# Eight chunk sums of a conditioning matrix moved from TensorE to VectorE, other quarters of the PE array for odd 64x64 matrices, and new woven orders, in a two-block fp32 trunk

## The reference, cut to what matters

```python
shift, scale, gate = jnp.split(jax.nn.silu(c) @ p['w_ada'] + p['b_ada'], 3, axis=-1)
shift_c, scale_c, gate_c = jnp.split(jax.nn.silu(c_ctx) @ p['w_ada'] + p['b_ada'], 3, axis=-1)
h = x * (1.0 + scale[:, None, :]) + shift[:, None, :]
...
sol = lax.linalg.triangular_solve(eye + lmat, rhs, left_side=True, lower=True, unit_diagonal=True)
```

## Time and profile before

| | |
|---|---|
| median of 3 runs | 1589.13 us (1587.75 to 1591.42) |
| profiled execution, its own time | 1589.21 us |
| its span in the profile | 1587.4 us |
| granted TensorE clock over the span | 0.997 |
| TensorE busy | 1547.7 us, 97% |
| VectorE / ScalarE / GpSimd busy | 612.0 / 390.3 / 198.6 us |

### The profile page before, as it was taken

How to read it: one execution, slowest core, us unless ns; L and a number is a source line. 1 busy time by engine, 2 the same in 40 slices (tenths; PEclk the granted TensorE clock), 3 DMA queues, 4 the chain that set the end, 5 groups by cost and what they waited for, 6 DMA issues and landing times.

```text
span 1587.4 us, 18219 instructions
## 1 busy us (share of the span) xinstructions
PE 1547.7 (97%) x7512; PEld 1017.6 (64%) x7512; DVE 612.0 (39%) x1394; ACT 390.3 (25%) x750; POOL 198.6 (13%) x274
## 2 busy tenths in 40 slices
PE   6999999999999999999999999999999999999997
PEld 2544544455444444464876888588888858889873
DVE  1332433464100001423344412265678216567721
ACT  1122325323100000031226320144223213422320
POOL 0321200221010011113011202110100011010000
PEclk9999999999999999999999999999999999999999
DMA  8732222302022222241331243424221434232231
GB/s 356 271 158 106 107 106 106 133 27 79 1 80 79 80 106 92 80 178 53 129 134 63 102 183 134 153 107 155 107 108 55 161 121 154 107 130 85 88 125 40
DMA packets 17366, 184.16 MB, mean 116 GB/s; under 512 B 2306, under 2 KB 2818, under 8 KB 4740
## 3 DMA queue, kind: packets, MB, share of 16 engines
q1 hardware_dynamic: 17284, 183.01, 30.3%
HBM read 181.95 MB, written 1.05 MB: 115 GB/s over the span
## 4 chain that ended last, share of the span: by engine, by line
PE 95%; ACT 3%; DVE 1%; DMA 1%; issue 1%; SPq 0%; POOLq 0%; POOL 0%; ACTq 0%
PE ps L688 91%; PE ps L743 3%; DMA arena<-in_wf 1%; DVE arena L1613 0%; ACT arena L1227 0%; ACT L1567 0%; ACT L1565 0%; DVE arena L1610 0%; DVE arena L1607 0%; ACT arena L1440 0%; ACT arena L1565 0%; ACT arena L1456 0%; ACT L1458 0%; ACT L1456 0%; ACT arena L1567 0%
## 5 line engine op out<-in xcount | busy, mean ns | idle before, releaser
L688 PE MATMUL ps<-arena 128*128 128x256 f32 (+9 forms) x7020 | 1498.9, 398 | 27.6 <-DMA arena<-in_wf 11.2
L688 PEld LDWEIGHTS ps<-arena 128*128 128x128 f32 (+6 forms) x7020 | 963.8, 177 | 529.3 <-issue 422.6
L2161 POOL TENSOR_TENSOR arena<-arena 128x256 f32<-128x256 f32 (+5 forms) x214 | 164.0, 786 | 936.0 <-DVE arena L1613 575.9
L1613 DVE SCALAR_TENSOR_TENSOR arena<-arena 128x256 f32<-128x256 f32 (+4 forms) x455 | 212.9, 524 | 139.5 <-ACT arena L1369 38.8
L1613 DVE SCALAR_TENSOR_TENSOR arena<-arena,ps 128x256 f32<-128x256 f32 (+2 forms) x136 | 64.6, 482 | 397.7 <-PE ps L688 292.7
L1227 ACT ACTIVATE arena<-ps 128x512 f32<-128x512 f32 (+2 forms) x216 | 110.0, 523 | 354.3 <-PE ps L688 315.4
L1607 DVE TENSOR_TENSOR arena<-arena 128x512 f32<-128x512 f32 (+14 forms) x156 | 92.1, 612 | 115.2 <-ACT arena L1227 39.9
L743 PEld LDWEIGHTS ps<-arena 128*128 128x128 f32 x488 | 55.8, 141 | 30.4 <-issue 20.5
L1395 ACT ACTIVATE arena<-ps 128x512 f32<-128x512 f32 (+1 forms) x24 | 13.5, 562 | 248.5 <-PE ps L688 248.5
L743 PE MATMUL ps<-arena 128*128 128x128 f32 x488 | 71.3, 277 | 3.2 <-ACT arena L1474 1.5
L1610 DVE TENSOR_SCALAR arena<-arena 128x256 f32<-128x256 f32 (+9 forms) x181 | 62.9, 383 | 15.7 <-POOL arena L2161 10.8
(11 more groups left out here) (92 smaller groups left out, 289.5 us busy)
## 6 DMA issues: line engine op xcount, KB each, us to landing
arena<-in_wf SPq DMA_DIRECT2D x69, 2048.0 KB, 8.1
arena<-in_wf SPq DMA_DIRECT2D x22, 1024.0 KB, 6.9
arena<-in_wf SPq DMA_DIRECT2D x2, 1152.0 KB, 7.8
arena<-in_xinT SPq DMA_DIRECT2D x2, 1024.0 KB, 16.1
arena<-in_xin SPq DMA_DIRECT2D x4, 512.0 KB, 3.9
arena<-in_rp SPq DMA_DIRECT2D x2, 1024.0 KB, 8.5
arena<-in_consts SPq DMA_DIRECT2D x1, 1410.0 KB, 19.1
arena<-in_pa SPq DMA_DIRECT2D x2, 532.0 KB, 10.0
```

Source lines behind the costliest of these rows:

```text
L688: return e.matmul(o, l, r, start=start, stop=stop, skip_group_check=True)
L1613: return e.scalar_tensor_tensor(out=o, in0=x, scalar=s, in1=y, op0=op0, op1=op1)
L2161: return e.tensor_tensor(o, x, y, op)
```

## The change

1. The products of the later eight ada pieces leave TensorE. VectorE multiplies each of the 8 chunks of a piece (128x512) by a per-partition scalar and adds it up, for each of the two rows: 16 instructions for a piece, 2 `tensor_scalar` and 14 `scalar_tensor_tensor`, into `ACC`, four tiles of 128x512 in `X`. They are cut into four parts of four instructions (`ep`), put into the four steps after the place where `ef` stood. TensorE turns the four blocks of both sums (`es`, `et`: 8 transposes for a piece where there were 4), two pieces later; VectorE reduces and adds the bias once for each row. ScalarE's copy goes. The weights of the piece are done with only when VectorE's last part is.
2. In the inverse, odd matrices use the other two quarters of the array (upper rows to lower outputs and the reverse) and a second PSUM bank, so four matmuls on four quarters follow each other. Fourteen of the sixteen groups of a layer are so changed (t0 to t5, y0 to y3, x0 to x3). Each copy and each predicated copy becomes two of 128x256 (or four of 64x256). Four matmuls of 128 columns with 64 stationary columns are added for the swapped halves of `wt`.
3. `ORDER_A[0]` and `ORDER_A[1]` are new strings with the same counts of letters. `ORDER_B` is unchanged.

```diff
 ORDER_A = [
-    "daadddddaaddaddddadadgaaadgadgaadgdgaagdagadagadgadagadgagadgaadgadaaggadaaaggadggaadggagadgagdgaaddgaggadgggaa"
-    "dgagdagdagdggadgdgaadgaagadagaagdadgaadgadagddaadaaaddaaadaagagadgaaaggagadgagagagadgadaggdaggggg",
+    "dddddddddaaddadadadadaagdggdagdddadgaadadgadaadaggaagaagdaagagdagadaggddgaaaaaggaadggadgadagaaggagdadgadaagag"
+    "adgagggdaaagggdgdaaaadgaagdaaagdgdadagdaadagddaadaddggagdgagagagadggaagagaadgaaggaadggaagggaggggd",
...
 def dense_a(l):
-        return ([("es", k - 1, "V")] if k else []) + ([("ef", k, "A")] if k < len(ADA_LATER) else [])
+        turn = [k - 2] if 2 <= k < 8 else [6, 7] if k == 8 else []
+        return [(n, i, "V") for i in turn for n in ("es", "et")] + ([("ef", k, "-")] if k < len(ADA_LATER) else [])
...
+    for i, step in enumerate(list(steps)):
+        for n, k, _ in step:
+            if n == "ef":
+                for q in range(4):
+                    steps[i + 1 + q] = steps[i + 1 + q] + [("ep", 4 * k + q, "-")]
+    steps = [[g for g in step if g[0] != "ef"] for step in steps]
...
             for n, (l, j) in enumerate(ADA_LATER):
-                out[f"a{l}ada{j}"] = dense_done(0, "ef", n)
+                out[f"a{l}ada{j}"] = ada_acc.at(0, n)
...
                 b = bank("wt", l)
                 for d in range(2):
                     p.wait_ge(de_iv.at(l, IV_W + d))
+                    for j in range(2):
+                        mm(b[HALVES[j], 256 + 128 * d:384 + 128 * d], W16[:, d, 4 - 4 * j:8 - 4 * j, :], ident, d == 0, True)
...
+                def quarters(o):
+                    return [(o + n, HALVES[j], HALVES[1 - j if n else j]) for n in range(2) for j in range(2)]
...
-                        b = bank("y", l, k)
-                        for i in range(8):
-                            for x in HALVES:
-                                ins = mm(b[x, 64 * i:64 * i + 64], NL[x, 8 * d + i, x], XM64[x, 8 * d + i, :], i == 0, True)
+                        b = [bank("y", l, k, n) for n in range(2)]
+                        for i in range(4):
+                            for o, x, z in quarters(8 * d + 2 * i):
+                                ins = mm(b[o % 2][z, 64 * i:64 * i + 64], NL[x, o, x], XM64[x, o, :], i == 0, True)
...
+            def ada_parts(k, q):
+                l, j = ADA_LATER[k]
+                w = weights(f"a{l}ada{j}", 8)
+                v.wait_ge(pieces[f"a{l}ada{j}"][2], dense_dve(0, "ps", 3))
+                if k > 1 and q == 0:
+                    v.wait_ge(dense_done(0, "et", k - 2))
+                for kk in (2 * q, 2 * q + 1):
+                    for r in range(2):
+                        acc = ACC[k % 2][r]
+                        if kk == 0:
+                            ins = ts(acc, w[:, kk, :], cs3[:, kk, r:r + 1], None, ALU.mult)
+                        else:
+                            v.wait_ge(acc_made[r])
+                            ins = stt(acc, w[:, kk, :], cs3[:, kk, r:r + 1], acc, ALU.mult, ALU.add)
...
-                        copy(Y64[:, 8 * d:8 * d + 8, :], r3(psum("y", l, k), 8)).then_inc(de_yc.hit(l, k), 1)
+                        for n in range(2):
+                            ins = copy(Y64[:, 8 * d + n:8 * d + 8:2, :], r3(psum("y", l, k, n)[:, 0:256], 4))
+                        ins.then_inc(de_yc.hit(l, k), 1)
...
```

More of the change, by code:

```diff
@@ L209, in build_program @@
         PT4 = [X[:, 0:512], X[:, 512:1024]]
+        ACC = [[X[:, 1024 * i + 512 * r:1024 * i + 512 * r + 512] for r in range(2)] for i in range(2)]
         cs3 = r3(cs, 8)
@@ L341, in after @@
         def after(e, *per):
-            return Ev(e.sem, *per, start=sum(e.per))
+            return Ev(e.sem, *per, start=e.base[0] + sum(e.per))
         def landed(e, l=0):
@@ L349, in build_program @@
         pt_zero = after(cs_ready, 2)
+        ada_acc = ev("ada_acc", 8)
         DENSE = [dense_a(l) for l in range(2)]
-        FLAT = [[g for step in s for g in step if g[0] != "hx"] for s in DENSE]
+        FLAT = [[g for step in s for g in step if g[0] not in ("hx", "ep")] for s in DENSE]
         FIRST = [("pf", 0, "A"), ("pf", 1, "A"), ("ps", 0, "V"), ("ps", 1, "V"), ("pf", 2, "A"), ("pf", 3, "A"),
@@ L1104, in delta @@
                         p.wait_ge(de_yc.at(l, k), de_tc.at(l, k))
-                        b = bank("x", l, k)
-                        for i in range(8):
-                            for x in HALVES:
-                                ins = mm(b[x, 64 * i:64 * i + 64], XT64[x, 8 * d + i, :], Y64[x, 8 * d + i, :], i == 0, True)
+                        b = [bank("x", l, k, n) for n in range(2)]
+                        for i in range(4):
+                            for o, x, z in quarters(8 * d + 2 * i):
+                                ins = mm(b[o % 2][x, 64 * i:64 * i + 64], XT64[z, o, :], Y64[z, o, :], i == 0, True)
                         ins.then_inc(de_x.hit(l, k), 1)
@@ L1115, in delta @@
                 yield
-                b = bank("y", l, 4)
+                b = bank("y", l, 4, 0)
                 for i in range(8):
@@ L1123, in delta @@
                 p.wait_ge(de_yc.at(l, 4), de_tc.at(l, 5))
-                b = bank("x", l, 4)
+                b = bank("x", l, 4, 0)
                 for i in range(8):
@@ L1547, in delta @@
                 a.wait_ge(de_y.at(l, 4))
[L1548 removed]
+                copy(Y64[:, 0:8, :], r3(psum("y", l, 4, 0), 8)).then_inc(de_yc.hit(l, 4), 1)
                 yield
@@ L1624, in ada_sum, with ada_turned @@
                     ).then_inc(dn_dve.hit(0, BY_DVE[0][(g, n)]), 1)
+            acc_made = [None, None]
+            def ada_parts(k, q):
[12 more added lines that the diff above has]
+                            ins = stt(acc, w[:, kk, :], cs3[:, kk, r:r + 1], acc, ALU.mult, ALU.add)
+                        if (kk, r) != (7, 1):
+                            ins.then_inc(v.own(), 1)
+                            acc_made[r] = v.now()
+                        else:
+                            ins.then_inc(ada_acc.hit(0, k), 1)
+            def ada_turned(k, r):
+                l, j = ADA_LATER[k]
+                g = ("es", "et")[r]
+                v.wait_ge(dense_done(0, g, k), landed(d_bada, l))
+                a4 = AS[:, 4 * r:4 * r + 4]
+                e.tensor_reduce(a4, r3(psum("dense", 0, g, k), 4), AX, ALU.add).then_inc(v.own(), 1)
+                v.wait_ge(v.now())
+                stt(r3(SCOL[l], 24)[:, 4 * j:4 * j + 4, r], a4, 1.0 if j in (2, 3) else 0.0,
+                    BADA[:, 24 * l + 4 * j:24 * l + 4 * j + 4], ALU.add, ALU.add
+                    ).then_inc(dn_dve.hit(0, BY_DVE[0][(g, k)]), 1)
+                v.wait_ge(dense_dve(0, g, k))
             def dense(l):
```

102 lines of the change are left out of this document (53 added, 49 removed).

## The result

The changed kernel takes **1592.97 us** (median, 1590.57 to 1595.44) beside 1588.85 of the kernel before on the same chip: ratio 1.0026, interval 1.0018 to 1.0035. It is slower by 4.1 us, just over what such a measurement tells from no change. The prediction said 1584, faster by some 5 us. Its range holds the result; its likeliest case and its direction do not.

The account below looks back on a forecast made before the run. It took TensorE's work, busy 1547.7 of 1587.4 us, plus few idle stretches as the bound. Terms -10 + 10 - 0.5 - 5.4 = -5.9 us gave 1583.3, rounded to 1584; 8-in-10 range 1574 to 1597 us.

Parts of the forecast that it names:

- likeliest case: Whole kernel: all terms as forecast, 1584 us, faster than before; chance 0.48.
- 3. Orders: Layer A0's new strings: some idle may go, the new tail waits some 1.5 us; -0.5 us for both.
- The bound of +2: Upper bound in us for `ORDER_A[1]`, said only to permute work in which TensorE hardly idles; lower bound -1, taken as 0.
- The ada products, -10 us: TensorE in A0: eight pieces' products go, 14.6 us, and 32 transposes are added, 4.7 us; work falls by 10 us.
- VectorE's sums, +10 us: A0: later ring loads make TensorE wait before gg, su and sv; at least 7.0 us, at most 20, taken as +10.
- The chain there is load, TensorE, load: Why A0's added load waits would hide against nothing else; used for the +10 us of VectorE's sums.
- forecast 12.0: A0: next piece's load lands 12.0 us behind the TensorE group, after VectorE's part (2.5 us) and the load (8.1 us).
- forecast 9.8: A0, ag to gg: TensorE's letters between the last ag group and the gg piece take 9.8 us.
- The quarters, -5.4 us: Inverses of two layers: four quarters at work shorten the groups, net of wt's added matmuls; -2.7 us a layer.
- The first rival: Inverse: two quarters still set the pace, +2 in place of -5.4 us, 1591 us; chance 0.2.
- its 0.49: Inverse: time in us of a 32-record group with four quarters, taken from bounds 0.49 and 0.98.
- The second rival: A0: VectorE's order sets the pace, price 20 us in place of 10, 1594 us; chance 0.2.

Follow-up runs that it names:

- the third run: The changed kernel without its quarters (VectorE's sums and new orders, inverse as before): 1599.67 us, ratio 1.0075 to the kernel before.
- the fourth: The kernel before with the new ORDER_A strings alone: 1604.79 us, ratio 1.0107 to the kernel before.
- the fifth run: The changed kernel with VectorE's part moved ahead of the projection group's item in its step: 1588.05 us, ratio 0.9999 to the kernel before.
- the first experiment: The kernel before with the inverse's quarters alone, products and orders as before: 1579.51 us, ratio 0.9953; repeated later, 1581.48 us.

## Why the prediction was wrong

It had the kernel faster by 5.9 us; it is slower by 4.1. The step that failed is "**3. Orders**", -0.5 us.

- **The orders, -0.5 us: the step that failed.** They cost 17.0 us alone. The sentence costed the two ends of the string and never asked what covers the letters where projections are moved away from between them. A TensorE record in such a run was priced by its pace where it was covered, and the wait for ScalarE's copy (0.6 us in the earlier trace rows, with both hand-overs about 0.8) was left out. The bound of +2 was too narrow for the same reason.
- **The clock: no term at all.** In the profiled run A0's stretches at 1.2 GHz cost an estimated 5.6 us, and all lie in or behind short waits. Spans multiplied by their granted clock are 1582.2 us in the mean of the changed kernel's executions and 1581.0 to 1582.0 for the kernel before on the three chips of the experiments. By this estimate the two would be level at the full clock, and nearly all of the 4.1 us is the clock's.
- **The ada products, -10 us: right.** A0's TensorE work fell by 9.3 us, or by 11.2 when the 1.9 us of longer busy time that the orders alone bring are set apart.
- **VectorE's sums, +10 us: too high, and by another mechanism.** On the new orders the sums save 5.1 us net, so they cost some 5 or 6: idle of A0 is 17.0 us in the third run against 11.3 in the fourth. "The chain there is load, TensorE, load" is the sentence that does not hold. Behind the last ag group the load landed 12.9 us later (forecast 12.0), but TensorE was still at the letters for 15.6 us. Without its 4.0 us of idle and the half clock it would have been through in about 9.5 (forecast 9.8). VectorE's order and the clock came in ahead of the load. For sums on the old orders the chain of loads is real (41.0 us of load waits).
- **The quarters, -5.4 us: right mechanism, size short.** They bring 7.5 us alone, 7.8 on top of the rest. A layer's first stretch, t0 to x1, went from 5.74 to 4.12 us (1.6, forecast 1.5), y2 to y4 from 8.55 to 6.36 (2.2, forecast 1.9), wt cost 0.64 (forecast 0.65), and an idle of 0.69 us at 1184 that the forecast let stand is gone too. The first rival fell: one group takes 0.47 to 0.55 us, not 0.98. The rule cited from the Trainium skill (TensorE: Matmul & The Clock Gate, The mechanism), that a load overlaps matmuls in flight only with another row group, does not pace this case. The forecast's own reason was weak, though: 0.081 and 0.075 us against 0.109 are 1.3 and 1.5 times the single pace, not twice, so its 0.49 was a better guess than its rows bore out.
- **The sum.** Without the quarters, -0.5 was forecast (-10 + 10 - 0.5); the runs give +11.6 (4.1 + 7.5). The orders miss by 17.5, and sums that cost less than forecast hide about 5 of it; the clock is in both. That the result lies in the range owes much to this and to the quarters. The second rival's 1594 is near in time by luck: 11.3 of the 17.1 us of idle are there without any sums on VectorE, and VectorE ends only half of it. At gg its mechanism is there (VectorE's part, then the letters), but its 15.8 us for VectorE's letters and the measured 15.6 are not the same sum.

## What to carry to other kernels

An order string is a resource: a projection between two dependent small steps is what hides their hand-over, so price every place from which one is taken away, at the hand-over's full length and with the clock that may fall behind it. An engine that is busy half of the time as one half of a ping-pong may have no room in its gaps; put work where it waits for something that is late anyway (the sums of the first piece, the part ahead of the multiply). And undo each part of a change alone: here one part of three carried all of the gain.

## What was not expected of the hardware

- The clock fell to 1.2 GHz in or behind waits that are short each: at 165.1, behind 0.32 and 0.57 us and within the 3.12 us that begin at 164.5; at 301.6, behind 0.83, 1.48, 0.49, 0.64 and 0.96 us (at 293 to 302); at 352.8, behind 0.85, 1.34 and 0.44 us (at 348 to 352). It need not fall: the fourth run's profile has 0.83, 1.48 and 1.35 us within 9 us at 300 and keeps the full clock through A0. Filling the wait of 3.12 us with idle work kept the clock full there; the kernel was then some 3 us faster, which the intervals leave likely rather than shown.
- Four 64*64 quarters with two loads in each row group run at about twice the pace of two (0.47 to 0.55 us a group of 32 records, against 0.98).
- The four scalar-tensor-tensor operations of a part took 3.85 us with GpSimd at work on its own (from 161.72 us, a row of eight operations) and 2.73 us without it in the fifth run. The Trainium skill (Advanced Engine Details and Errata, GPSIMD Details) says that GpSimd shares a read and a write interface with VectorE and conflicts with operations that have two inputs in SBUF, as these have; the trace agrees. GpSimd's eight operations took 6.68 us there and 5.20 in the fifth run. The forecast had 2.5 us for the part.
- In the changed kernel's inverses TensorE stood still for 0.95 and 0.79 us inside x1 for nothing that the profile shows ("issue"); the first experiment, with the same inverse, has neither. This was not explained.
